# Compression with three products for two neighbouring blocks, x normalized beside it, and a later wait for projection's stores

## Time and profile before

| what | us |
|---|---|
| median of 3 runs | 2632.16 (2631.3 to 2635.83) |
| profiled execution | 2622.21 |
| its span | 2620.2 |
| TensorE busy | 2160.3 (82%) |
| VectorE busy | 441.0 (17%) |
| ScalarE busy | 246.7 (9%) |
| GpSimd busy | 108.0 (4%) |
| mean granted TensorE clock | 0.899 |

### The profile page before, as it was taken

The page is one execution under the profiler, slowest core; times in us unless marked ns, Lnnn a source line. Parts: engine busy times, 40 slices in busy tenths (PEclk is TensorE's granted clock), DMA queues, the critical chain, the costliest instruction groups (busy, mean ns, idle before and its releaser), DMA issues. The chain is left out here.

```text
span 2620.2 us, 33664 instructions
## 1 busy us (share of the span) xinstructions
PE 2160.3 (82%) x13995; PEld 1339.8 (51%) x13995; DVE 441.0 (17%) x1052; ACT 246.7 (9%) x650; POOL 108.0 (4%) x124
## 2 busy tenths in 40 slices
PE   8999399999976999996877788899994577777773
PEld 7888267777756766664444344576332223322321
DVE  0000010002571121221112111111004111111112
ACT  0000110001210021211001000100001000000000
POOL 0000000000000000000000000000001111112211
PEclk9999699998985999998898988899996788888986
DMA  5552623332323332332999999843327899999998
GB/s 201 145 153 88 243 81 115 126 126 83 113 96 110 109 112 93 101 104 97 413 412 413 407 410 413 333 164 116 116 74 289 340 406 409 413 409 407 401 410 336
DMA packets 130950, 614.69 MB, mean 235 GB/s; under 512 B 29716, under 2 KB 34085, under 8 KB 93157
## 3 DMA queue, kind: packets, MB, share of 16 engines
q1 hardware_dynamic: 107166, 561.97, 55.4%
q0 software_dynamic: 22800, 45.07, 4.8%
q10 hardware_dynamic: 856, 5.77, 0.5%
HBM read 702.95 MB, written 39.60 MB: 283 GB/s over the span
## 5 line engine op out<-in xcount | busy, mean ns | idle before, releaser
L423 PE MATMUL bank<-ut,wring 128*128 128x320 f32 x1408 | 382.6, 433 | 0.0
L423 PEld LDWEIGHTS bank<-ut,wring 128*128 128x128 f32 x1408 | 267.3, 191 | 110.4 <-issue 1.3
L686 PE MATMUL bank<-ut,wring 128*128 128x320 f32 x1024 | 303.0, 442 | 16.9 <-ACT selmask L849 15.0
L686 PEld LDWEIGHTS bank<-ut,wring 128*128 128x128 f32 x1024 | 191.3, 193 | 93.5 <-issue 27.3
L1938 PE MATMUL bank<-wdn,par 128*32 128x512 f32 x512 | 91.3, 849 | 110.1 <-issue 108.9
L1380 PE MATMUL bank<-wring,arena 128*128 128x512 f32 x256 | 118.4, 605 | 3.1 <-DVE arena L1417 1.6
L1909 PE MATMUL bank<-wgu,arena 128*32 128x512 f32 x1024 | 118.4, 602 | 0.8 <-DVE arena L1989 0.8
L247 PE MATMUL bank<-arena,wring 128*128 128x256 f32 x512 | 115.9, 389 | 2.1 <-DMA arena<-in_cmp_kv 2.1
L558 DVE RECIPROCAL snew<-snew 128x320 f32<-128x320 f32 x30 | 64.5, 2149 | 314.0 <-ACT snew L527 314.0
L247 PE MATMUL bank<-zt,wring 128*128 128x256 f32 x512 | 111.8, 379 | 0.0
L247 PEld LDWEIGHTS bank<-arena,wring 128*128 128x128 f32 x512 | 99.9, 196 | 16.4 <-DMA arena<-in_cmp_kv 2.2
(11 more groups left out here) (394 smaller groups left out, 2077.7 us busy)
## 6 DMA issues: line engine op xcount, KB each, us to landing
wgu<-in_w_gu SPq DMA_DIRECT2D x128, 1024.0 KB, 17.0
wdn<-in_w_dn SPq DMA_DIRECT2D x32, 2048.0 KB, 25.1
wring<-in_w_proj SPq DMA_DIRECT2D x44, 1024.0 KB, 4.8
arena<-in_kv_k SPq DMA_DIRECT2D x64, 640.0 KB, 10.2
arena<-in_kv_v SPq DMA_DIRECT2D x64, 640.0 KB, 17.0
wring<-in_w_gate SPq DMA_DIRECT2D x32, 1024.0 KB, 5.1
wring<-in_w_merge SPq DMA_DIRECT2D x32, 1024.0 KB, 4.8
wring<-in_kv_k SPq DMA_DIRECT2D x32, 640.0 KB, 15.8
```

The costliest lines, as they stand in the source:

```text
L423: last = nc.tensor.matmul(m.bank[:, 2 + s % 2, 0:T], m.wring[:, s, k * P:(k + 1) * P], m.ut[:, k, :], start=(k == 0), stop=(k == KD - 1))
L686: last = nc.tensor.matmul(m.bank[:, 6 + n % 2, 0:T], m.wring[:, n % 3, k * P:(k + 1) * P], m.ut[:, k, :], start=(k == 0), stop=(k == KD - 1))
```

## The change

1. Two sequences and one kind make a unit (8 units: pair 0 k, pair 0 v, pair 1 k, ...). Blocks are numbered even and odd (E_m, O_m). Window 2m is `E_m W0 + O_m W1`, window 2m+1 is `O_m W0 + E_(m+1) W1`. The kernel now computes three products: `O (W0 + W1)`, `(E_next - O) W1` and `(E - O) W0`. The first plus the third is `O W1 + E W0`, the first plus the second is `O W0 + E_next W1`. Each is a chain of 16 matmuls with 256 columns, where the columns are two sequences x 16 pages x 2 groups x 4 blocks. VectorE makes the sums of weights once per kind and the differences for each unit (`ahead` in `m.vt`, the other in place). Each page's cache is laid out anew on the host: k and v apart, even and odd blocks apart. A page's DMA is 128 KB, 1 KB per partition. SyncE loads the first sequence of a pair, ScalarE the second.
2. x is loaded straight into `m.ut` during compression. ScalarE squares a quarter of it (4 x 320 elements per partition) in each of units 2 to 5, after that unit's gelu; TensorE adds it up one unit later (4 matmuls); VectorE scales `m.ut` in place in unit 7. Projection's slots 0 and 1 are loaded after unit 6. The small product moves behind projection's first four products.
3. The wait for the six stores moves from the end of projection's SyncE queue to the end of the prompt stage's.

The diff, cut to its core:

```diff
+        def load(eng, u, e):
+            pair, kv = u // 2, u % 2
+            for pg in range(PAGES):
+                v = eng.value_load(m.pages[0:1, (2 * pair + e) * PAGES + pg:...], min_val=0, max_val=NPHYS - 1)
+                if pg == 0 and u >= 2:
+                    eng.wait_ge(pre_done, u - 1)
+                eng.dma_start(rows[u % 2][:, e * PAGES + pg, :, :, :].rearrange("p i e n -> p (i e n)"),
+                              a["cmp_kv"][bass.ds(v, 1), kv, :, :].rearrange("o p n -> (o p) n")
+                              ).then_inc(rows_in[u % 2], 16)
 @block.sync
+            load(sp, 0, 0)
             sp.dma_start(... a["w1_v"]).then_inc(m.w1_in[1], 16)
+            load(sp, 1, 0)
+            for c in range(4):
+                sp.dma_start(m.ut[:, 4 * c:4 * c + 4, :], a["x_t"][:, 4 * c:4 * c + 4, :]).then_inc(m.small_in, 16)
+            for u in range(2, NU):
+                load(sp, u, 0)
+            sp.wait_ge(pre_done, NU - 1)
+            for s in range(2):
+                sp.dma_start(m.wring[:, s, :], a["w_proj"][s, :, :]).then_inc(m.w_in[s], 16)
 @block.tensor
+            position(0)
+            for u in range(NU):
+                kv, s = u % 2, u % 2
+                pe.wait_ge(w_sum_ready, kv + 1)
+                pe.wait_ge(rows_in[s], 512 * (u // 2 + 1))
+                if u >= 2:
+                    pe.wait_ge(sum_ready, u - 1)
+                chain(m.bank[:, s, 0:256], w_sum[kv], [rows[s][:, :, l, 1, :] for l in range(HALF)])
+                if u == 0:
+                    position(1)
+                if u >= 2:
+                    second(u - 2)
+                pe.wait_ge(diff_ready, 2 * u + 1)
+                chain(m.bank[:, 2 + s, 0:256], w1[kv][:, HALF:CBLK, :], [ahead[:, l, :, :] ...]).then_inc(ahead_read, 1)
+                pe.wait_ge(diff_ready, 2 * u + 2)
+                chain(m.bank[:, s, 256:512], w1[kv][:, 0:HALF, :], [rows[s][:, :, l, 0, :] ...]).then_inc(pre_done, 1)
+                if u - 1 in NORM_AT:
+                    pe.wait_ge(sqx_ready, r + 1)
+                    (4 matmuls of m.c("ones") with sqx[r % 2] into bank 7)
+            second(NU - 2)
+            second(NU - 1)
 @block.scalar
+            load(act, 0, 1)
+            load(act, 1, 1)
+            for u in range(NU):
+                if u + 2 < NU:
+                    load(act, u + 2, 1)
+                act.wait_ge(sum_ready, u + 1)
+                nc.scalar.activation(hid[:, u % 2, :], ..., ACT.Gelu_apprx_tanh, ...).then_inc(act_ready, 1)
+                if u in NORM_AT:
+                    nc.scalar.activation(sqx[r % 2], m.ut[:, 4 * r:4 * r + 4, :], ACT.Square).then_inc(sqx_ready, 1)
+                if u == 6:
+                    act.wait_ge(norm_done, 4)
+                    nc.scalar.activation(rs, m.bank[:, 7, 0:T], ACT.Sqrt, ...).then_inc(rs_ready, 1)
 @block.vector
+            def differences(u):
+                dve.wait_ge(rows_in[u % 2], 512 * (u // 2 + 1))
+                if u:
+                    dve.wait_ge(ahead_read, u)
+                for g in range(G):
+                    tensor_tensor(out[:, :, :, g, 0:3], even[:, :, :, g, 1:4], odd[:, :, :, g, 0:3], ALU.subtract)
+                for e in range(2):
+                    last = tensor_tensor(out[:, c, :, :, 3], even[:, nxt, :, :, 0], odd[:, c, :, :, 3], ALU.subtract)
+                last.then_inc(diff_ready, 1)
+                dve.wait_ge(diff_ready, 2 * u + 1)
+                tensor_tensor(r[:, :, :, 0, :], r[:, :, :, 0, :], r[:, :, :, 1, :], ALU.subtract).then_inc(diff_ready, 1)
+            for u in range(NU):
+                if u:
+                    sums(u - 1)
+                differences(u)
+                if u == 0:
+                    weights(1)
+                if u >= 2:
+                    keep(u - 2)
+                if u == 7:
+                    (wait rs_ready; reciprocal; 16 scalings of m.ut)
+            keep(NU - 2)
+            sums(NU - 1)
+            keep(NU - 1)
 project_stage, sync: slots 2 and 3 first, then small weights and cosines
-            sp.wait_ge(m.stores, 6 * 16)
 project_stage, tensor
             for s in range(SLOTS):
                 product(s, s)
+            (small product)
 prompt_stage, sync, at its end
+            sp.wait_ge(m.stores, 6 * 16)
```

More of the change, by code:

```diff
@@ L235, in position @@
                 last.then_inc(pos_done, 1)
-            def hidden(i, s, kv):
-                first = isinstance(i, int)
-                if kv == 0:
[L240 to L250, removed]
@@ new lines, in chain @@
+            def chain(out, w, src):
+                for l in range(HALF):
+                    last = nc.tensor.matmul(out, w[:, l, :], src[l], start=(l == 0), stop=(l == HALF - 1))
+                return last
+            position(0)
[7 more added lines that the diff above has]
+                if u == 0:
+                    position(1)
+                if u >= 2:
+                    second(u - 2)
+                pe.wait_ge(diff_ready, 2 * u + 1)
+                chain(m.bank[:, 2 + s, 0:256], w1[kv][:, HALF:CBLK, :], [ahead[:, l, :, :] for l in range(HALF)]
+                      ).then_inc(ahead_read, 1)
+                pe.wait_ge(diff_ready, 2 * u + 2)
+                chain(m.bank[:, s, 256:512], w1[kv][:, 0:HALF, :], [rows[s][:, :, l, 0, :] for l in range(HALF)]
+                      ).then_inc(pre_done, 1)
+                if u - 1 in NORM_AT:
+                    r = NORM_AT[u - 1]
+                    pe.wait_ge(sqx_ready, r + 1)
+                    for k in range(4):
+                        last = nc.tensor.matmul(m.bank[:, 7, 0:T], m.c("ones"), sqx[r % 2][:, k, :],
+                                                start=(r == 0 and k == 0), stop=(r == 3 and k == 3))
+                    last.then_inc(norm_done, 1)
@@ L292, in _ @@
                 act.wait_ge(pos_done, kv + 1)
[L293 to L301, removed]
+                nc.scalar.activation(m.posc[:, kv:kv + 1], m.bank[:, 6 + kv, 0:1], ACT.Copy).then_inc(act_ready, 1)
@@ L303, in _ @@
         @block.vector
         def _(dve):
[L305 to L313, removed]
@@ L428, in _ @@
                 product(s, s)
+            pe.wait_ge(csw_in, 32)
+            for k in range(KD):
+                last = nc.tensor.matmul(m.bank[0:64, 1, 0:T], wsmall[:, k, :], m.ut[:, k, :],
+                                        start=(k == 0), stop=(k == KD - 1))
+            last.then_inc(small_done, 1)
             with pe.Fori(1, 7) as i:
```

198 lines of the change are left out of this document (97 added, 101 removed).

## The result

The changed kernel takes 2519.43 us in the median of 4 runs (2513.05 to 2521.35), the kernel before 2633.99 us (2631.3 to 2637.37). The ratio is 0.956, with a 95% interval of 0.9539 to 0.9582: 114.6 us less.

The account below looks back on a forecast made before the run. Compression was taken as bound by TensorE's matmuls, followed by a 71 us chain that nothing overlaps. Gains of 108.1 + 6.4 = 114.5 us gave 2507.7 profiled, 2518 in the median; forecast 2508 to 2529, range 2507 to 2541.

Parts of the forecast that it names:

- Three products: Compression: three matmul chains instead of four take 55.9 us off TensorE; the next stage begins at 227.0, not 273.3.
- the tail: Compression's end, from the last chain to the next stage: 6.3 us, where it was 3.2 before.
- What hides VectorE: Compression: VectorE's 11.2 to 12 us per unit hide under TensorE's 21; cost zero to 0.3 us a unit, taken as zero.
- Loads: Compression: a unit's rows land 20.2 us after their buffer is free, needed at 21; cost zero, margin under 2 us.
- the upper bound of 117 ns: Compression's row loads: a 1 KB row costs at most a 2 KB row's 117 ns per engine, 30 us for 256 rows.
- The normalization's chain: Between compression and projection: the whole chain from 273.3 to 344.2 goes; 108.1 us net, including the saving in compression.
- Slots beside the copies: Projection's start: slots 2 and 3 load beside GpSimd's two copies; stall of 0 to 3 us, taken as zero.
- Stores: End of projection: the 8.1 us wait goes and the prompt stage's product runs earlier; gain 6.4 us, bounds 0 and 8.1.
- Rival (a): Compression: row loads bind, costing about 4L - 89 us for L us per four megabytes; 2529 to 2561 us, chance 0.14.
- L + 21: Compression, if row loads bind: time of each of three later pairs of units instead of 44 us; L loads four megabytes.
- The sum: Whole kernel: 108.1 us up to projection's first product plus 6.4 us at the prompt stage's start, 114.5 us.

Follow-up runs that it names:

- the fourth chain: Changed kernel with each unit's middle chain made twice, the second time into a spare place; 2574.6 us, first projection product 58.3 us later.
- the delay experiment: Changed kernel with three unneeded VectorE additions of 1024 elements between sums and differences in units 1 to 7; 2536.8 us.
- The two norm experiments: Changed kernel with x loaded and normalized behind the last unit, without and with GpSimd's two copies issued at that moment; 2529.8 and 2556.5 us.
- the experiment: Changed kernel with the wait for the six stores put back at the end of projection's SyncE queue; 2525.1 us.

## Why the prediction was right

- *Three products.* Right. Unit 0 was forecast to end at 59.8 (60.0), the units to take 21, 21.9 and 24.1 us (20.7, 21.6, 23.7), the last chain to end at 220.7 (218.9) and the first product to start at 227.4 (224.6). That unit 0 came to 0.2 us is luck, since the same code ended it anywhere from 59.9 to 64.1. The second products cost the 0.9 us that was taken. A chain costs 6.91 us from start to start where 6.99 was taken, which is nearly all of the 1.8 us at the last chain's end; the tail was 1.0 us shorter than forecast. That TensorE binds was argued from its busy share and is shown by the fourth chain.
- *What hides VectorE.* Right in size: differences ready 6.4 us after a unit's end, covered by 7.0 and a second product. It was closer than 12 busy us of 21 suggest, and the delay experiment put the price of a miss on record. It also showed that a wait of 3.3 us cost some 3 us more than itself, at the lower clock.
- *Loads.* Right for two queues: 16.3 to 17.3 us of issue, then 2.8 in the median to land. So 256 rows passed an engine in about 20 us, under 80 ns each (an estimate from these rows), and the upper bound of 117 ns was not reached. The rate follows the issues, so the row's own price stays open.
- *The normalization's chain.* Right. Parts 1 and 2 together gained, net of the small product, 110.4 us (119.6 less 9.2), forecast 108.1. The size was known because a chain that nothing overlaps goes as a whole. The two norm experiments show that the copies were its largest part.
- *Slots beside the copies.* Forecast 0, bound 3. Slot 3 took 24.4 us from its issue, the small weights 32.2: by bytes 27 and 36 were forecast, by row count 17. The packet-wise turn that I had cited from the Trainium skill, "DMA: Bandwidth & Descriptors", section "Queues, rings and completion order", would, as I read it, have meant the latter; here a megabyte took 18.9 us (from slot 2's landing to slot 3's) and half a megabyte with as many rows 8.3. So the share went by bytes, and the trace does not bear out that reading. No stall came at slot 3 because it landed 1 us before its product; the cosines came 0.4 us late.
- *Stores.* Forecast 6.4, measured 5.6 (5.0 by the experiment). Constants were forecast to land about 10 us after the stage's start, and did at 10.4. The product behind them came 14.8 us from the last rotation, where 14.0 was forecast.
- *Rival (a)* failed in its price at 38 us: 63 us forecast for one queue, 102 measured. The failed term is L + 21, 59 us for a pair of units: it takes the loads of both buffers to run side by side, and one queue needs two times 35.
- The sum was 114.5 us, the medians give 114.6. The parts miss by +2 and -1 us, and for the profiled execution 2507.7 was forecast and 2513.05 measured, most of it in the experts' stage. What makes the agreement of the medians better than that is luck, as single executions scatter by more.

## What to carry to other kernels

A stretch in which every engine waits in turn is the safest thing to count: it goes whole, and what is left is the work that has to stand somewhere else. Next to it, ask for each transfer what else moves data at the same moment; here two background copies decided 25 us in one place and some 26 in another. And a second issuing queue doubles the rate of small loads only where issue time is the bound, which the issue rows show directly (16 loads in about 17 us at 128 KB as at 256 KB).

## What the runs showed of the hardware

- The price of issuing a row load with its page number read from SBUF hardly depended on its size: 16 loads of 256 KB took SyncE 17.0 to 18.9 us in the kernel before, 16 loads of 128 KB took 16.7 to 17.3 on SyncE and 16.3 to 17.0 on ScalarE in the changed kernel, side by side. One queue took 34.5 to 34.8 us for 32.
- During the 32 one-column matmuls in a row of unit 0 the granted clock fell (0.63 and 0.82 of full speed in their stretch, in two runs of the same compression code); in three runs with the same matmuls between 256-column ones it stayed at 1.00. The first such row of each kernel took 13.8 us against 8.6 to 11.3 for the second, at a listed clock of 1.00; no run here says why. A wait of 3.3 us was followed by a chain that took 10.2 us instead of 7.1, at a granted clock of 0.50 for 5.5 us.
- Beside a background copy between two places of HBM, SyncE's loads came at 1 MB in 18.9 us and 0.5 MB in 8.3; slot 2, issued before the copy had begun, took 5.9. Another queue did not help the constants behind the stores: 10.4 us from issue to landing on SyncE's, 11.0 on ScalarE's.
